# Decay levels of the third block: affine step of the forget gate inside the logarithm, row copy one place forward, signed differences

## The chip, the cores and the metric

The kernel runs on one core of a Trainium2 chip. The metric is the device time of one execution in microseconds; before the change it is 2814.32 us (median of 3 runs, 2813.81 to 2816.1).

## The reference, cut to what matters

Three model blocks run one after the other over 1024 tokens of width 1024. The change lies in the HGRN2 mixer of the third: four heads, each 128 channels by 1024 tokens.

```python
forget = lbf + (1.0 - lbf) * jax.nn.sigmoid(f_pre)
log_f = jnp.log(forget)
k = 1.0 - forget
b = jnp.cumsum(log_f, axis=2)                     # inside a chunk
diff = b[:, :, :, None, :] - b[:, :, None, :, :]
decay = jnp.exp(jnp.where(causal[:, :, None], diff, -jnp.inf))
scores = jnp.einsum('bhtd,bhsd,bhtsd->bhts', qc, kc, decay)
o = jnp.einsum('bhts,bhse->bhte', scores, vc) + jnp.einsum('bhtd,bhde->bhte', qc * jnp.exp(b), S)
S = jnp.exp(b_last) * S + jnp.einsum('bhsd,bhse->bhde', kc * jnp.exp(b_last - b), vc)
```

The decay depends on the channel, so the scores are not one plain matmul. The kernel works with chunks of 128 tokens and splits the pairs (query t, key s) by levels. At level j the tokens fall into groups of 2m, m = 2^j. A key in the first half of a group meets a query in its second half through the pivot, the last token of the first half: exp(b[t]-b[s]) = exp(b[t]-pivot) * exp(pivot-b[s]). Both exponents are at most zero.

## The kernel before, in words

The third block multiplies h3 (1024 tokens) by its weights in 16 channel tiles, called windows w = 0 to 15 here. A window is 16 steps of three matmuls (lines 369 to 371: high by high, low by high, high by low part), each 128x128 by 512. Its result is copied out of PSUM by ScalarE with Copy, Silu or Sigmoid (line 2614). Window 5 + 2h yields the sigmoid of head h, tile `p3[FT3 + h]`. ScalarE then makes the high part of the weights of window w + 2 (`high`, line 2569) and GpSimd the low part (`low`, line 2410).

From window 7 on, TensorE puts one item of the decay work after every third step, five to a window. The items are listed in `items`: for each of the four heads "diag", the levels 0 to 6, "end" and "start", 40 in all. Level 0 has m = 1 and level 6 has m = 64. I call the point of TensorE's order at which item n stands its slot. Each engine goes through the items in an order written out in the code, with semaphores between them:

- VectorE, loop of lines after `cumulate(0)`: for n = 0, 1, ... it does `difference(n)` (line 2704), `queries_decayed(n - 1)` (line 2718: query half times its exponential) and `merge(n - 3)` (lines 2728 and 2736: the scores in PSUM are copied by mask into `score`). In the turn of level 6 it also does `forget` of the next head (lines 2676 and 2681) and in the turn of "start" `cumulate` (line 2687, eight prefix sums of 128 tokens).
- ScalarE: in window w it does `exponents(n)` for five items, two ahead of TensorE's: a pass Abs (line 2576) and a pass Exp with scale -1 (line 2578) over the same tile `dec_e`. After the first of them comes the logarithm (line 2607) of the next head. `rows` (line 2591) copies the transposed keys of "end" from PSUM over the head's decay tile. Then it waits for the end of the window and does line 2614 and `high`.
- GpSimd: `low`, then `keys_decayed(n)` (line 2421: key half times its exponential).
- TensorE: `level(n)` (line 2466 for levels, 2464 for "diag", 2462 for the transposes of "end"). It waits for the keys, the queries and, since items n and n - 2 use the same PSUM pair, for `merge(n - 2)`, and after an "end" for `rows`.

`dec_e` has four buffers (`difference(n)` waits for the matmuls of item n - 4), `qe` has three.

```python
nc.scalar.activation(e, e, ACT.Abs).then_inc(abs_ok, 1)
act.wait_ge(abs_ok, upto(n, has_diff))
nc.scalar.activation(e, e, ACT.Exp, scale=-1.0).then_inc(exp_ok, 1)
```

Of the kernel before, what the change touches and what calls it, by code (L numbers as in the profile page):

```python
# [10 lines left out]
ACT = mybir.ActivationFunctionType  # L11
ALU = mybir.AluOpType
# [3 lines left out]
P = 128  # L16
S = 1024
# [61 lines left out]
def build(nc, a, out):  # L79
# [4 lines left out]
    def sem(name):  # L84
        held.append(nc.alloc_semaphore(name))
        return held[-1]
# [14 lines left out]
    with top:  # L101
# [2183 lines left out]
        def first_of_third(sp):  # L2285
            for n in range(2):
# [10 lines left out]
                    bias=(at(169, "bo2", [P, D]), a["b_out2"]),  # L2297
# [6 lines left out]
        p3 = at(16, "p3", [P, 2 * KT, S])  # L2304
# [4 lines left out]
        lbs = at(4.25, "lbs", [P, 8, 4])  # L2309
# [12 lines left out]
        kT3 = at(128, "kT3", [P, 2, S])  # L2322
# [14 lines left out]
        QT, FT3, GT = 4, 8, 12  # L2337
        N_T3, N_J3, LOOK, PER_TILE = 2 * KT, 3 * KT, 2, 5
        kinds = ["diag"] + list(range(LEVELS)) + ["end", "start"]
        items = [(h, kind) for h in range(HEADS) for kind in kinds]  # L2340
        N_ITEM3, FIRST_WINDOW = len(items), 7

        def upto(n, which):
            return sum(which(kind) for _, kind in items[:max(0, n + 1)])

        is_level = lambda kind: isinstance(kind, int)
        has_diff = lambda kind: is_level(kind) or kind == "end"
# [26 lines left out]
        def half_slot3(x, n):  # L2374
# [3 lines left out]
        p3_lbs, tile3_mm, p3_out, w3_hi, w3_lo, i_mm, i_out = (sem(x) for x in (  # L2378
            "p3_lbs", "tile3_mm", "p3_out", "w3_hi", "w3_lo", "i_mm", "i_out"))
        c3_in, win_step, lb_dve, lb_act = sem("c3_in"), sem("win_step"), sem("lb_dve"), sem("lb_act")  # L2380
        zero_ok, forget_ok, ln_ok, cum_ok = sem("zero_ok"), sem("forget_ok"), sem("ln_ok"), sem("cum_ok")
        diff_ok, abs_ok, exp_ok, qe_ok, ke_ok, lv_mm, merged, rows_ok = (sem(x) for x in (
            "diff_ok", "abs_ok", "exp_ok", "qe_ok", "ke_ok", "lv_mm", "merged", "rows_ok"))
        el_ok, o3_mm, st3_mm, st3_ok, sq3_ok, sd3_ok, on3_ok, ot3_mm, y3_ok, own3 = (sem(x) for x in (
            "el_ok", "o3_mm", "st3_mm", "st3_ok", "sq3_ok", "sd3_ok", "on3_ok", "ot3_mm", "y3_ok", "own3"))
        pool_mm, pool_ok = sem("pool_mm"), sem("pool_ok")
# [5 lines left out]
        with nc.Block() as block:  # L2392
# [47 lines left out]
            def _(pe):  # L2440
                def level(n):
                    h, kind = items[n]
                    if not has_mm(kind):
                        return
                    bank = pair[2 + n % 2]
                    if upto(n - 2, is_score):
                        pe.wait_ge(merged, upto(n - 2, is_score))
                    ends = upto(n - 2, lambda x: x == "end")
                    if ends:
                        pe.wait_ge(rows_ok, ends)  # L2450
                    if kind == "diag":
                        pe.wait_ge(forget_ok, 2 * h + 2)
                    else:
                        pe.wait_ge(ke_ok, upto(n, has_diff))
                    if is_level(kind):
                        pe.wait_ge(qe_ok, upto(n, by_q))
                    e = dec_e[:, n % N_DEC, :]
                    for c in range(TT):
                        tok = slice(c * P, (c + 1) * P)
                        o = bank[:, c // 4, c % 4 * P:(c % 4 + 1) * P]  # L2460
                        if kind == "end":
                            last = nc.tensor.transpose(o, e[:, tok], ident[:])
                        elif kind == "diag":
                            last = nc.tensor.matmul(o, kT3[:, h % 2, tok], queries(n)[:, tok], start=True, stop=True)
                        else:
                            last = nc.tensor.matmul(bank[:, 0, c * 64:(c + 1) * 64], e[:, tok],
                                                    qe[:, n % N_QE, c * 64:(c + 1) * 64], start=True, stop=True)
                    last.then_inc(lv_mm, 1)
# [24 lines left out]
                for w in range(2, N_T3):  # L2493
                    pe.wait_ge(w3_lo, w + 1)
                    pe.wait_ge(p3_out, w - 1)
                    for i in range(2 * KT):
                        tile_step(w, i)
                        n = PER_TILE * (w - FIRST_WINDOW) + i // 3
# [63 lines left out]
            def _(act):  # L2562
# [8 lines left out]
                def exponents(n):  # L2571
                    h, kind = items[n]
                    e = dec_e[:, n % N_DEC, :]
                    if has_diff(kind):
                        act.wait_ge(diff_ok, upto(n, has_diff))
                        nc.scalar.activation(e, e, ACT.Abs).then_inc(abs_ok, 1)
                        act.wait_ge(abs_ok, upto(n, has_diff))
                        nc.scalar.activation(e, e, ACT.Exp, scale=-1.0).then_inc(exp_ok, 1)
                    elif kind == "start":
                        act.wait_ge(cum_ok, h + 1)  # L2580
                        b = decay(n)
                        nc.scalar.activation(elast[:, h, :], b.rearrange("p (c s) -> p c s", s=P)[:, :, P - 1],
                                             ACT.Exp).then_inc(el_ok, 1)
                        act.wait_ge(lv_mm, upto(n - N_DEC, has_mm))
                        nc.scalar.activation(e, b, ACT.Exp).then_inc(exp_ok, 1)

                def rows(n):
                    act.wait_ge(lv_mm, upto(n, has_mm))
                    act.wait_ge(el_ok, head_of(n) + 1)
                    act.wait_ge(exp_ok, upto(n + 1, has_exp))  # L2590
                    nc.scalar.activation(decay(n), flat(pair[2 + n % 2]), ACT.Copy).then_inc(rows_ok, 1)
# [8 lines left out]
                for w in range(N_T3):  # L2600
                    h = (w - 6) // 2
                    starts = w >= 6 and w % 2 == 0 and h < HEADS
                    todo = items_in(w)
                    for i, n in enumerate(todo):
                        if starts and (h == 0 and i == 0 or h and i == 1):
                            act.wait_ge(forget_ok, 2 * h + 2)
                            nc.scalar.activation(p3[:, FT3 + h, :], p3[:, FT3 + h, :], ACT.Ln).then_inc(ln_ok, 1)
                        exponents(n)
                        if n >= 3 and items[n - 3][1] == "end":
                            rows(n - 3)  # L2610
                        if n == N_ITEM3 - 1:
                            rows(n - 1)
                    act.wait_ge(tile3_mm, w + 1)
                    nc.scalar.activation(p3[:, P3_ORDER[w], :], flat(p3_pair(w)),
                                         (ACT.Copy, ACT.Silu, ACT.Sigmoid, ACT.Silu)[P3_ORDER[w] // 4]).then_inc(p3_out, 1)
                    high(w + 2)
# [6 lines left out]
                for c in range(TT):  # L2623
# [9 lines left out]
                    if c < 4:  # L2633
                        act.wait_ge(pool_mm, c + 1)
                        nc.scalar.activation(y3T[:, c, :], flat(pair[3]), ACT.Copy,
                                             scale=col("pool_scale", c)).then_inc(pool_ok, 1)

            @block.vector
            def _(dve):
                second_out[3](dve)  # L2640
                own = Count(dve, lb_dve)
# [9 lines left out]
                own.then(nc.vector.reciprocal(lbs[:, 4, :], lbs[:, 3, :]))  # L2651
                own.then(nc.vector.tensor_tensor(lbs[:, 5, :], lbs[:, 1, :], lbs[:, 4, :], ALU.mult))
                own.then(nc.vector.tensor_scalar(lbs[:, 6, :], lbs[:, 5, :], -1.0, 1.0, ALU.mult, ALU.add))
                step = Count(dve, win_step)
                dve.wait_ge(c3_in, 48)
                for g, w in enumerate(POOL_WINDOWS):
                    x = p3[:, g, :]
                    dve.wait_ge(p3_out, g + 1)
                    step.then(nc.vector.tensor_copy(win[0][:, 16:], x))
                    m, i = 1, 0  # L2660
                    while m < w:
                        step.then(nc.vector.tensor_tensor(win[1 - i][:, 16:], win[i][:, 16:],
                                                          win[i][:, 16 - m:16 + S - m], ALU.add))
                        m, i = 2 * m, 1 - i
# [8 lines left out]
                def forget(h):  # L2673
                    f = p3[:, FT3 + h, :]
                    dve.wait_ge(p3_out, 6 + 2 * h)
                    nc.vector.tensor_scalar(f, f, lbs[:, 6, h:h + 1], lbs[:, 5, h:h + 1], ALU.mult,
                                            ALU.add).then_inc(forget_ok, 1)
                    dve.wait_ge(forget_ok, 2 * h + 1)
                    if h >= 2:
                        dve.wait_ge(lv_mm, upto((h - 1) * len(kinds) - 1, has_mm))  # L2680
                    nc.vector.tensor_scalar(kT3[:, h % 2, :], f, -1.0, 1.0, ALU.mult, ALU.add).then_inc(forget_ok, 1)

                def cumulate(h):
                    f = p3[:, FT3 + h, :]
# [9 lines left out]
                def difference(n):  # L2694
                    h, kind = items[n]
                    if not has_diff(kind):
                        return
                    m = 1 << kind if is_level(kind) else P
                    size = 2 * m if is_level(kind) else P
                    b = decay(n).rearrange("p (c s) -> p c s", s=size)  # L2700
                    e = dec_e[:, n % N_DEC, :].rearrange("p (c s) -> p c s", s=size)
                    if upto(n - N_DEC, has_mm):
                        dve.wait_ge(lv_mm, upto(n - N_DEC, has_mm))
                    nc.vector.tensor_tensor(e, b, b[:, :, m - 1:m].broadcast_to([P, S // size, size]),
                                            ALU.subtract).then_inc(diff_ok, 1)

                def queries_decayed(n):
                    h, kind = items[n]
# [34 lines left out]
                for n in range(N_ITEM3 + 3):  # L2743
# [6 lines left out]
                    h, i = (n + 3) // len(kinds), (n + 3) % len(kinds)  # L2750
# [986 lines left out]
def rows(w):  # L3737

    k, n = w.shape
    return np.ascontiguousarray(w.reshape(k // P, P, n).transpose(1, 0, 2))  # L3740
# [101 lines left out]
```

## Time and profile before

| what | value |
|---|---|
| median of 3 runs | 2814.32 us |
| profiled execution, its time | 2812.37 us |
| its span | 2810.5 us |
| TensorE busy | 2706.1 us, 96% |
| VectorE busy | 2108.7 us, 75% |
| ScalarE busy | 1035.8 us, 37% |
| GpSimd busy | 489.2 us, 17% |
| mean granted TensorE clock | 0.991 |

TensorE is busy nearly all the time over the whole span. The busy time of a matmul is modelled: matmuls overlap, so that one of 0.39 us follows the one before after 0.23 us. What is worth reading are the stretches in which TensorE is idle, and how far apart its pieces of work start. The decay items run from 1810 us to 1969 us.

### The profile page before, as it was taken

The numbers are of one execution on the slowest core, as the hardware profiler recorded it, in microseconds if no ns is written. First come the engines' busy times: TensorE is split into PE (matmuls) and PEld (weight loads), VectorE is DVE, ScalarE is ACT, GpSimd is POOL, SyncE is SP. The second block draws the span as 40 slices with busy tenths as digits, with TensorE's granted clock in tenths as the row PEclk, the third lists the DMA queues.
The fourth block names the chain that finished last, engine by engine and source line by source line (L and its number), as shares of the span: only waits on it lengthen the run. The fifth ranks groups of instructions, "written<-read, shape, count | busy, mean of one in ns | idle before, by whom it ended". The sixth has DMA issues, their size and how long they took to land. (4 is left out here: it accounts for less than half of the span.)

```text
span 2810.5 us, 33531 instructions
## 1 busy us (share of the span) xinstructions
PE 2706.1 (96%) x13192; PEld 2204.2 (78%) x13192; DVE 2108.7 (75%) x2827; ACT 1035.8 (37%) x1500; POOL 489.2 (17%) x260
## 2 busy tenths in 40 slices
PE   6999999999999999899999899999999999999998
PEld 5888888888888878488776578878878788888887
DVE  6999997864724672599977876688186988887978
ACT  5111112142414332422127641477231555545332
POOL 0000000000100011002220100345120466665000
PEclk8999999999999999999999999999999999999999
DMA  5212322233335551011110032110122222224431
GB/s 222 113 61 74 107 81 62 90 109 122 111 107 170 151 164 53 31 61 45 46 57 2 31 126 96 39 31 20 57 107 88 83 83 90 75 90 165 188 98 60
DMA packets 97567, 250.19 MB, mean 89 GB/s; under 512 B 7345, under 2 KB 34353, under 8 KB 95746
## 3 DMA queue, kind: packets, MB, share of 16 engines
q1 hardware_dynamic: 92866, 231.49, 24.2%
q10 hardware_dynamic: 4288, 15.73, 1.4%
q8 instruction: 105, 1.72, 0.3%
q0 software_dynamic: 256, 0.82, 0.1%
q14 instruction: 52, 0.43, 0.1%
HBM read 202.92 MB, written 45.09 MB: 88 GB/s over the span
## 5 line engine op out<-in xcount | busy, mean ns | idle before, releaser
L369 PE MATMUL pair<-u_hi,w_hi 128*128 128x512 f32 x768 | 302.1, 393 | 1.2 <-PEq L92 0.9
L640 DVE SCALAR_TENSOR_TENSOR conv_acc<-aT,cols,conv_acc 128x1024 f32<-128x1024 f32 x232 | 297.8, 1283 | 6.7
L370 PE MATMUL pair<-u_lo,w_hi 128*128 128x512 f32 x768 | 300.2, 391 | 0.0
L371 PE MATMUL pair<-u_hi,w_lo 128*128 128x512 f32 x768 | 300.1, 391 | 0.0
L369 PEld LDWEIGHTS pair<-u_hi,w_hi 128*128 128x128 f32 x768 | 145.1, 189 | 32.6 <-issue 2.4
L1867 DVE TENSOR_SCALAR_CACHE_REDUCE counted<-choice,top_i 128x384 uint8<-128x384 f32 (+2 forms) x192 | 169.2, 941 | 0.0
L370 PEld LDWEIGHTS pair<-u_lo,w_hi 128*128 128x128 f32 x768 | 145.1, 189 | 30.6 <-issue 0.7
L371 PEld LDWEIGHTS pair<-u_hi,w_lo 128*128 128x128 f32 x768 | 145.0, 189 | 30.6
L369 PE MATMUL pair<-h_hi,ch_hi 128*128 128x512 f32 x392 | 155.4, 396 | 2.2 <-ACT ch L1763 2.0
L370 PE MATMUL pair<-h_lo,ch_hi 128*128 128x512 f32 x392 | 153.2, 391 | 0.0
L371 PE MATMUL pair<-h_hi,ch_lo 128*128 128x512 f32 x392 | 153.1, 391 | 0.0
L1013 POOL TENSOR_TENSOR yrT<-yrT,gate_c 128x1024 f32<-128x1024 f32 x8 | 18.9, 2369 | 758.2 <-ACT yrT L906 758.2
L3033 POOL TENSOR_TENSOR op_lo<-w_sum,op_hi 128x512 fp32r<-128x512 f32 x80 | 137.0, 1713 | 34.2 <-ACT op_hi L3163 34.2
L1652 POOL TENSOR_TENSOR ch_lo<-wt,ch_hi 128x1024 fp32r<-128x1024 f32 x17 | 40.9, 2404 | 526.4 <-ACT ch_hi L1611 526.4
L453 DVE TENSOR_TENSOR w_lo<-wt,w_hi 128x1024 fp32r<-128x1024 f32 (+1 forms) x64 | 69.8, 1090 | 77.1 <-ACT w_hi L449 77.1
L3083 PE MATMUL pair<-t_hi,op_hi 128*128 128x512 f32 x320 | 124.6, 389 | 0.1
L3085 PE MATMUL pair<-t_lo,op_hi 128*128 128x512 f32 x320 | 124.5, 389 | 0.0
L3086 PE MATMUL pair<-t_hi,op_lo 128*128 128x512 f32 x320 | 124.5, 389 | 0.0
L449 ACT ACTIVATE w_hi<-wt 128x1024 fp32r<-128x1024 f32 (+1 forms) x64 | 60.8, 950 | 142.8 <-PE pair L371 135.1
L1272 DVE TENSOR_TENSOR wo_lo<-wo_raw,wo_hi 128x1024 fp32r<-128x1024 f32 x44 | 54.1, 1229 | 66.7 <-ACT wo_hi L1401 66.6
L369 PE MATMUL pair<-h_hi,p_hi 128*128 128x512 f32 x256 | 103.5, 404 | 0.0
L371 PE MATMUL pair<-h_hi,p_lo 128*128 128x512 f32 x256 | 100.2, 391 | 0.0
(497 smaller groups left out, 7041.0 us busy)
## 6 DMA issues: line engine op xcount, KB each, us to landing
wt<-in_w_ch SPq DMA_DIRECT2D x60, 512.0 KB, 3.4
wo_raw<-in_w_out SPq DMA_DIRECT2D x44, 512.0 KB, 3.6
wt<-in_w_up SPq DMA_DIRECT2D x10, 1024.0 KB, 4.9
w_raw<-in_w_up SPq DMA_DIRECT2D x10, 1024.0 KB, 4.9
g_spill<-g_stage SPq DMA_DIRECT2D x40, 256.0 KB, 2.2
ada_mod<-in_ada_mod SPq DMA_DIRECT2D x4, 2048.0 KB, 14.4
wt<-in_w_conv SPq DMA_DIRECT2D x16, 512.0 KB, 3.5
qk<-qk_st SPq DMA_DIRECT2D x8, 1024.0 KB, 6.4
```

The source lines that it names most:

```text
L369: nc.tensor.matmul(bank, w[0], x[0], start=(first and k == 0), stop=False)
L370: nc.tensor.matmul(bank, w[0], x[1], start=False, stop=False)
L371: return nc.tensor.matmul(bank, w[1], x[0], start=False, stop=(last and k == n_k - 1))
L449: nc.scalar.activation(slot_view(w_parts[0], n), slot_view(wt, n), ACT.Copy).then_inc(job_hi, 1)
L453: nc.vector.tensor_tensor(slot_view(w_parts[1], n), slot_view(wt, n), slot_view(w_parts[0], n).bitcast(F32), ALU.subtract).then_inc(job_lo, 1)
L640: nc.vector.scalar_tensor_tensor(dst, x, w, conv_acc[:], ALU.mult, ALU.add).then_inc(conv_step, 1)
L1272: nc.vector.tensor_tensor(wo_parts[1][:, n % 2, :], wo_raw[:, n % 2, :], wo_parts[0][:, n % 2, :].bitcast(F32), ALU.subtract).then_inc(wo_ ...
L1867: nc.vector.tensor_scalar(counted[:, t % 2, 0:w], scores(t), least, None, op, ALU.add, accum_out=found[:, t - 2:t - 1]).then_inc(counts_ok, 1)
L3033: nc.gpsimd.tensor_tensor(op_lo[j], operand(w, j), op_hi[j].bitcast(F32), ALU.subtract).then_inc(op_lo_ok, 1)
L3083: nc.tensor.matmul(bank, hi[:, k, :], x_hi[:, k, :], start=(j in opens and k == 0), stop=False, skip_group_check=True)
L3085: nc.tensor.matmul(bank, hi[:, k, :], x_lo[:, k, :], start=False, stop=False, skip_group_check=True)
L3086: last = nc.tensor.matmul(bank, lo[:, k, :], x_hi[:, k, :], start=False, stop=(k == 3), skip_group_check=True)
```

## The change

- `forget` no longer writes the forget gate back. It computes only the keys, k = 1 - forget, as one affine step of the sigmoid with two columns per head (a new column `lbs[:, 7]` is the negative of `lbs[:, 6]`). The affine step of the forget gate itself is the scale and bias of the logarithm's activation.
- `rows` of the item "end" stands after the exponents two items later instead of three.
- `difference` writes the two halves of a group with separate instructions: pivot minus b for the keys' half, b minus pivot for the queries' half. "end" has the first only, over whole chunks. So the Abs pass goes, and Exp is taken without a scale.

```diff
@@ TensorE, level(n)
                     if kind == "diag":
-                        pe.wait_ge(forget_ok, 2 * h + 2)
+                        pe.wait_ge(keys_ok, h + 1)
@@ ScalarE, exponents(n)
                         act.wait_ge(diff_ok, upto(n, has_diff))
-                        nc.scalar.activation(e, e, ACT.Abs).then_inc(abs_ok, 1)
-                        act.wait_ge(abs_ok, upto(n, has_diff))
-                        nc.scalar.activation(e, e, ACT.Exp, scale=-1.0).then_inc(exp_ok, 1)
+                        nc.scalar.activation(e, e, ACT.Exp).then_inc(exp_ok, 1)
@@ ScalarE, windows
                         if starts and (h == 0 and i == 0 or h and i == 1):
-                            act.wait_ge(forget_ok, 2 * h + 2)
-                            nc.scalar.activation(p3[:, FT3 + h, :], p3[:, FT3 + h, :], ACT.Ln).then_inc(ln_ok, 1)
+                            act.wait_ge(keys_ok, h + 1)
+                            nc.scalar.activation(p3[:, FT3 + h, :], p3[:, FT3 + h, :], ACT.Ln, bias=lbs[:, 5, h:h + 1],
+                                                 scale=lbs[:, 6, h:h + 1]).then_inc(ln_ok, 1)
                         exponents(n)
-                        if n >= 3 and items[n - 3][1] == "end":
-                            rows(n - 3)
+                        if n >= 2 and items[n - 2][1] == "end":
+                            rows(n - 2)
@@ VectorE
                 own.then(nc.vector.tensor_scalar(lbs[:, 6, :], lbs[:, 5, :], -1.0, 1.0, ALU.mult, ALU.add))
+                own.then(nc.vector.tensor_scalar(lbs[:, 7, :], lbs[:, 6, :], -1.0, None, ALU.mult))
@@ VectorE, forget(h)
-                    nc.vector.tensor_scalar(f, f, lbs[:, 6, h:h + 1], lbs[:, 5, h:h + 1], ALU.mult,
-                                            ALU.add).then_inc(forget_ok, 1)
-                    dve.wait_ge(forget_ok, 2 * h + 1)
                     if h >= 2:
                         dve.wait_ge(lv_mm, upto((h - 1) * len(kinds) - 1, has_mm))
-                    nc.vector.tensor_scalar(kT3[:, h % 2, :], f, -1.0, 1.0, ALU.mult, ALU.add).then_inc(forget_ok, 1)
+                    nc.vector.tensor_scalar(kT3[:, h % 2, :], f, lbs[:, 7, h:h + 1], lbs[:, 6, h:h + 1], ALU.mult,
+                                            ALU.add).then_inc(keys_ok, 1)
@@ VectorE, difference(n)
-                    nc.vector.tensor_tensor(e, b, b[:, :, m - 1:m].broadcast_to([P, S // size, size]),
-                                            ALU.subtract).then_inc(diff_ok, 1)
+                    pivot = b[:, :, m - 1:m].broadcast_to([P, S // size, m])
+                    keys = nc.vector.tensor_tensor(e[:, :, 0:m], pivot, b[:, :, 0:m], ALU.subtract)
+                    if is_level(kind):
+                        keys = nc.vector.tensor_tensor(e[:, :, m:size], b[:, :, m:size], pivot, ALU.subtract)
+                    keys.then_inc(diff_ok, 1)
```

## Rows read from the trace of the kernel before

**Rows 1.** Busy time by stretch: us, then each engine's busy time (x instructions), clock.

```profile
1860.40:1902.00 41.60, 38.20 (x232) 32.79 (x232) 35.96 (x35) 31.28 (x30) 20.43 (x11) 1.00 0.09 26
1943.60:1967.50 23.90, 23.88 (x153) 21.42 (x154) 23.59 (x18) 16.07 (x16) 13.39 (x7) 1.00 0.04 12
1967.50:2000.00 32.50, 32.50 (x149) 26.97 (x147) 0.00 (x0) 7.29 (x9) 5.77 (x5) 1.00 0.11 34
```

**Rows 2.** TensorE's waits, 1700 to 2060 us: total us, times, longest.

```profile
PE pair L2466 <- POOL dec_e L2421: 2.7, 3, 0.9
PE pair L2462 <- POOL dec_e L2421: 2.6, 3, 0.9
PE pair L2466 <- DVE score L2736: 2.4, 3, 0.8
PE pair L2464 <- issue: 2.4, 3, 0.8
...
PE pair L2466 <- DVE score L2728: 0.4, 1, 0.4
```

**Rows 3.** TensorE's items of head 1 and two of head 2, in order of time.

```profile
1868.29 1.89 PE L2466 MATMUL pair<-qe,dec_e 128*128 128x64 f32 x16
1872.84 1.89 PE L2466 MATMUL pair<-qe,dec_e 128*128 128x64 f32 x16
1876.71 1.89 PE L2466 MATMUL pair<-qe,dec_e 128*128 128x64 f32 x16
1881.54 2.00 PE L2466 MATMUL pair<-qe,dec_e 128*128 128x64 f32 x16 [0.80 <-DVE score L2736]
1886.52 1.06 PE L2462 MATMUL pair<-ident,dec_e 128*128 128x128 f32 x8 [0.86 <-POOL dec_e L2421]
1893.19 2.02 PE L2464 MATMUL pair<-p,kT 128*128 128x128 f32 x16 [0.82 <-issue]
...
1902.06 1.97 PE L2466 MATMUL pair<-qe,dec_e 128*128 128x64 f32 x16 [0.90 <-POOL dec_e L2421]
```

**Rows 4.** Instructions by line: duration in ns, minimum, median and maximum, first and last start.

```profile
L2704 DVE TENSOR_TENSOR dec_e<-p x32: 1201/1272/3393, 1805.2 to 1957.6; 128x1024 f32<-128x1024 f32 x32
L2576 ACT ACTIVATE dec_e<-dec_e x32: 1043/1057/1065, 1806.5 to 1961.0; 128x1024 f32<-128x1024 f32 x32
L2718 DVE TENSOR_TENSOR qe<-p,dec_e x28: 677/693/1772, 1810.0 to 1960.9; 128x512 f32<-128x512 f32 x28
L2578 ACT ACT_TABLE_LOAD  x12: 1283/1283/1283, 1807.6 to 1958.4; - x12
L2676 DVE TENSOR_SCALAR p<-p,lbs x4: 811/2866/2874, 1798.9 to 1916.0; 128x1024 f32<-128x1024 f32 x4
L2681 DVE TENSOR_SCALAR kT<-p x4: 694/694/694, 1799.8 to 1918.9; 128x1024 f32<-128x1024 f32 x4
L2736 DVE COPY_PREDICATED score<-masks,pair x28: 697/730/1321, 1821.3 to 1966.6; 128x512 f32<-128x512 int32 x28
L202 ACT ACTIVATE xT<-xT,msum,g x8: 1224/1228/1233, 29.4 to 58.0; 128x1024 f32<-128x1024 f32 x8
```

**Rows 5.** ScalarE in order of time, head 0.

```profile
1815.47 1.06 ACT L2578 ACTIVATE dec_e<-dec_e 128x1024 f32<-128x1024 f32 x1
...
1830.73 1.02 ACT L2614 ACTIVATE p<-pair 128x1024 f32<-128x1024 f32 x1
```

**Rows 6.** VectorE in order of time, heads 0 and 1.

```profile
1840.63 4.76 DVE L2687 TENSOR_TENSOR_SCAN p<-ones_col,p 128x128 f32<-128x128 f32 x8
...
1862.92 1.31 DVE L2736 COPY_PREDICATED score<-masks,pair 128x512 f32<-128x512 int32 x1
...
1872.16 1.77 DVE L2718 TENSOR_TENSOR qe<-p,dec_e 128x512 f32<-128x512 f32 x1
```

**Rows 7.** GpSimd in order of time, heads 0 and 1.

```profile
1832.78 2.42 POOL L2410 TENSOR_TENSOR p_lo<-wt,p_hi 128x1024 fp32r<-128x1024 f32 x1 [0.98 <-ACT p_hi L2569]
...
1871.08 2.30 POOL L2421 TENSOR_TENSOR dec_e<-kT,dec_e 128x512 f32<-128x512 f32 x1 [1.13 <-ACT dec_e L2578]
```

More of the change, by code:

```diff
@@ L2380, in build @@
         c3_in, win_step, lb_dve, lb_act = sem("c3_in"), sem("win_step"), sem("lb_dve"), sem("lb_act")
-        zero_ok, forget_ok, ln_ok, cum_ok = sem("zero_ok"), sem("forget_ok"), sem("ln_ok"), sem("cum_ok")
-        diff_ok, abs_ok, exp_ok, qe_ok, ke_ok, lv_mm, merged, rows_ok = (sem(x) for x in (
-            "diff_ok", "abs_ok", "exp_ok", "qe_ok", "ke_ok", "lv_mm", "merged", "rows_ok"))
+        zero_ok, keys_ok, ln_ok, cum_ok = sem("zero_ok"), sem("keys_ok"), sem("ln_ok"), sem("cum_ok")
+        diff_ok, exp_ok, qe_ok, ke_ok, lv_mm, merged, rows_ok = (sem(x) for x in (
+            "diff_ok", "exp_ok", "qe_ok", "ke_ok", "lv_mm", "merged", "rows_ok"))
         el_ok, o3_mm, st3_mm, st3_ok, sq3_ok, sd3_ok, on3_ok, ot3_mm, y3_ok, own3 = (sem(x) for x in (
```

## The prediction

> **What bounds the kernel now.** First the page: TensorE is busy 96% of the span, so only what shortens TensorE's idle time or its work can move the end. Then the stretches [rows 1]. In one head's period of decay items (1860.4 to 1902.0 us) TensorE is busy 38.20 of 41.60 us. Before and after the items it is not idle at all: 32.50 of 32.50 us right behind them. The clock is 1.00 in these stretches, so no clock is to be won. In the same period VectorE is busy 35.96 us, ScalarE 31.28 and GpSimd 20.43. The waits [rows 2] put a bound on the whole change: TensorE waits 2.7 + 2.6 + 2.4 + 2.4 + 0.4 = 10.5 us in 13 places, and nowhere else among the decay items.
>
> The true price of a wait is read from the distances of the slots [rows 3]. An undisturbed item follows the one before after 3.87 us (1872.84 to 1876.71), and after 4.55 us where a window ends between them (1868.29 to 1872.84). Level 6 stands 4.83 us behind level 5: 0.96 late. "end" stands 4.98 us behind level 6: 1.11 late. "diag" stands 6.67 us behind "end", where 9 + 9 + 3 matmuls of 0.23 us (4.8) and the item's own 1.06 make 5.8: 0.85 late, and I give the item itself another 0.1 (2.02 us where 1.9 is normal). Level 1 costs 0.9 of wait and by the same refill 1.05. Together 4.05 us per head, so an undisturbed period is 37.5 us instead of 41.6. Three periods lie between level 1 of head 0 and of head 3: 12.2 us. Level 1 of head 0 has 0.4 of wait, 0.55 with refill. The last head from its level 1 on has no wait (23.88 of 23.90 busy). The most that can be had is 12.75 us.
>
> **The change part by part.** The times below are those of head 0, whose events recur 41.6 us later in head 1.
>
> *Abs pass.* It is 32 x 1.057 = 33.8 us of ScalarE [rows 4], an engine with 10 us to spare per head; as a sum it is worth nothing. Where it counts is the latency of the first items of a head. After the copy of a window and `high` comes Abs, then a table load (1.28 us), then Exp of level 1, starting at 1815.47 [rows 5]. VectorE and GpSimd both wait for it, and VectorE isn't idle again for 30 us. Without Abs the load directly follows `high` and Exp starts at 1814.41 and ends at 1815.47: 1.06 us earlier for everything behind. Table loads stay 12, as Exp still follows Copy or Ln.
>
> *Halved differences.* 28 of the 32 become two instructions of 512 elements. The trace has no such write. The nearest row is the query product, 512 elements with every second one read, 0.69 us, against 1.20 for a whole difference [rows 4]. Back to back each overlaps the next by about 0.08, so two cost 1.22 to 1.36, that is 0.05 to 0.15 more per level, and 7 x 0.1 = 0.7 us per head. The far end is `merge`: at the levels with m = 1 and 2 it takes 1.31 us for the same 512 elements, otherwise 0.70 [rows 4, 6]. If the strided write did that, levels 0 and 1 would cost 1.2 us more each, 2.4 us per head. I take the 0.1, since merge differs in more than its write (mask, PSUM). Below nothing: the halves cannot be faster than the whole, as the element count is the same.
> On this the Trainium skill, "SBUF — State Buffer", the box on SBUF cachelines, says that lines are 16 bytes and that fp32 may be strided by up to four elements without loss. By it halves with m = 1 and 2 are free of a penalty, and so should merge's writes be, at 1.31 us. By the rule the sum stays 12; with merge's price 1 to 3 us of it would go.
>
> *Two instructions, two chances to be cut off.* VectorE and GpSimd hold each other up here: a key product takes 2.30 us at 1871.08 and the query product that starts at 1872.16 takes 1.77 instead of 0.69 [rows 4, 6, 7]; the first waited for the difference, the second for the product. A halved difference lets a waiting key product in between its halves, which delays its Exp by one product (1.15 us), but the query product behind is then no longer held up. So it moves the wait, it does not add one.
> The same page of the Trainium skill ("Who interferes with whom") has it that whoever starts first holds the shared pair for its whole instruction, and that two-input instructions of VectorE take part. That speaks against the change, as it adds instructions on that pair; it is the first rival below.
>
> *Forget.* Line 2676 goes: 0.81 us alone, 2.87 beside GpSimd's `low` [rows 4]. What remains (line 2681) gets the columns as operands as 2676 had, so it costs 0.81 instead of 0.69, and it inherits the place behind `low` and its 2.87. So the gain is 0.69 us per head on VectorE, in the turn right before level 6. The extra small instruction at the start (`lbs` 7) runs on four columns once, while VectorE waits for windows: nothing; without that cover, under 0.2 us. Both ends for the keys: -0.69 and -0.6 us.
>
> *Ln with bias and scale.* An activation with both from columns takes 1.23 us (line 202) where a plain one takes 1.06 [rows 4]: +0.17 us per head on ScalarE, between Exp of level 6 and Exp of "end", where the removed Abs of "end" leaves 1.06. At worst it is 0.17 of 12.
>
> *Row copy.* It now waits right behind the Exp of "start" for the transposes of "end". Behind it on ScalarE stands Exp of the next head's level 0, whose difference comes 2 us later anyway. "diag" on TensorE waited for this copy ("issue" in [rows 2], 0.85 each); the copy stood behind level 0's Abs and Exp. That wait goes whole.
>
> **The walk through one head**, from Exp(1) ready at 1815.47, with these prices and one engine of the two held off as above. TensorE's undisturbed slots: level 1 at 1818.2, 2 at 1822.1, 3 at 1825.9, 4 at 1830.5, 5 at 1834.4, 6 at 1838.2, "end" 1842.1, "diag" of head 1 at 1848.0, level 1 of head 1 at 1855.7.
> VectorE: queries 1 and merge of "diag" to 1817.4 (TensorE needs it at 1818.2), difference 3 with a key product between its halves to 1819.8, queries 2 and merge 0 to 1821.5, difference 4 to 1823.3, queries 3 and merge 1 to 1825.0, difference 5 to 1826.8, queries 4 and merge 2 to 1828.0, difference 6 to 1830.2, queries 5 and merge 3 to 1831.4.
> ScalarE has Exp(5) done at 1827.9, then waits for the window (1828.3), copies it to 1830.2 (at 1830.73 to 1831.75 now, [rows 5]), `high` to 1831.2, Exp(6) to 1833.4.
> GpSimd does `low` from 1831.2 to 1833.6 (2.42, [rows 7]). The keys of head 1 wait for it: 1834.1. Key product 6 to 1835.3, difference of "end" to 1836.4, queries 6 and merge 4 to 1837.5. Level 6 can start at 1838.2: no wait. Merge 5 to 1838.1.
> ScalarE: Ln to 1836.0, load, Exp("end") to 1838.4 (1842.15 now). The key product of "end", 2.4 us like `low`, comes to 1841 with a scan in front: "end" at 1842.1, no wait. Prefix sums 4.76 us as now [rows 6]: 1842.9. Rows at 1843.2 to 1844.2, "diag" at 1848.0: no wait. "start" queries, merge 6, difference 0 to 1845.9; difference 1 to 1847.2; Exp(0) 1847.0; copy, `high`, load, Exp(1) of head 1 at 1852.6, three microseconds ahead of level 1's slot, as it was in head 0 (2.7).
> So every wait goes, with 0.2 to 1 us in hand at levels 1 and 6. The tightest is level 6, 0.7 us. I leave 0.75 us in all for places where it doesn't quite do: 12.0 us. The own time of the profiled execution, 2812.37 us, becomes 2800.4; the median shown is 1.95 us above it, so 2814.3 - 12.0 = 2802.3.
>
> **The rivals.**
> (A) The pair shared by VectorE and GpSimd becomes the bound. Per head, alone: differences 7 x 1.22 + 1.15, queries 7 x 0.61 + 1.15, keys 0.8, prefix sums 3.1, merges 6.5: 25.5 us of VectorE, of it 19 on the pair; GpSimd 7 x 1.15 + 2.4 + 2 x 2.4 = 15.2. That is 34.2 us of a 37.5 us period, 91%. For: little is left, and with merge's price on levels 0 and 1 it is 36.6. Against: the walk. Then a half to three quarters of the waits stay: 3 to 8 us gained, 2809 by the middle. 22%.
> (B) The engine gains are spent before TensorE sees them: POOL's latency decides at level 1 and "end". Against: ScalarE's Exp comes 1 and 4 us earlier. Gain under 3 us, or given back behind the items: 2813. 6%.
> (C) Slower: a halved difference costs as much as a whole one at every level (an instruction's price not falling with its size). Then VectorE has 7 x 1.15 = 8 us more per head on 35.96 busy of 41.6, less 0.7: 43.3, so the period grows by 1.7, in three heads 5 us: 2820. It decides from 0.95 us per half on, where the 0.69 of the query product speaks against it. 3%.
> (D) The change doesn't do what it says, for instance Exp needing more table loads: 2 or more further loads per head of 1.28 would bring ScalarE, 31.3 - 8.5 us busy, nowhere near the bound. In (B).
>
> **How the numbers follow.** Forecast 69%, its own range 2800.5 to 2805. (A) 22%, (B) 6%, (C) 3%. The range goes up to 2809 to hold most of (A), and down to 2800 (nothing beyond 12.75, and about 1.5 us for the runs). What a measurement can tell from no change is 0.2%, 5.6 us: a gain above it is the forecast, 69%, and three quarters of (A): 86%. Within it: the rest of (A), (B) and a part of (C), 11%. Slower 3%.
>
> **What would show it.** TensorE's waits on lines 2462, 2464 and 2466: under 1.5 us in all. Level 1 of head 0 to that of head 3: 112 to 113 us where it was 124.8 (three periods). No Abs; 60 differences, of 0.65 to 0.7 us alone; Ln near 1.2 us. The keys' step takes up to 2.9 us, 0.8 in head 0. Wrong: halves at levels 0 and 1 above 1.2 us, VectorE over 36 of its new period and TensorE still waiting at level 6 (then A), or a "diag" still late (then the rows' step).

## The result: 0.5% faster, more than forecast

| | before | changed |
|---|---|---|
| median of 4 runs | 2814.4 us (2813.81 to 2816.1) | 2798.69 us (2798.33 to 2800.32) |
| profiled execution | 2812.37 us | 2799.01 us |
| its span | 2810.5 us | 2796.6 us |
| TensorE busy | 2706.1 us | 2701.4 us |
| VectorE busy | 2108.7 us | 2102.8 us |
| ScalarE busy | 1035.8 us | 1003.9 us |

The ratio is 0.9947, 95% interval 0.9932 to 0.9962. The gain is 15.7 us by the medians, 13.9 us by the spans. The forecast was 12.0 us and 2802.3, range 2800.0 to 2809.0: the direction came out and so did the mechanism in the main; the time lies 1.3 us below the range, for reasons given behind the experiments.

The stretches of two heads, columns as in [rows 1]:

```profile
1855.30:1892.60 37.30, 37.30 (x233) 33.15 (x233) 34.73 (x41) 23.32 (x22) 19.41 (x10) 1.00 0.10 29
1892.60:1929.90 37.30, 37.30 (x234) 33.14 (x233) 34.72 (x41) 23.33 (x22) 18.50 (x11) 1.00 0.09 29
```

A head now takes 37.3 us instead of 41.6, and TensorE is busy in all of it, where it had 38.20 of 41.60 [rows 1]. ScalarE went from 31.3 to 23.3 us per head. VectorE went only from 36.0 to 34.7, so its share rose from 86% to 93%. TensorE's waits of the changed kernel from 1700 to 2060 us answer [rows 2]: no line of the decay items (2462, 2464, 2466) is left. The waits that are listed stand behind the items and are in the kernel before too, where they come 14 us later, so that part of them falls outside the window of [rows 2].

```profile
PE pair L2524 <- DVE y3T L2768: 3.1, 2, 2.7
PE pair L2543 <- DVE state L2778: 1.7, 2, 0.8
PE pair L369 <- PEq L2392: 1.1, 1, 1.1
```

TensorE's items of head 1 in order of time, which answer [rows 3]:

```profile
1863.08 1.89 PE L2466 MATMUL pair<-qe,dec_e 128*128 128x64 f32 x16
1867.63 1.89 PE L2466 MATMUL pair<-qe,dec_e 128*128 128x64 f32 x16
1871.50 1.89 PE L2466 MATMUL pair<-qe,dec_e 128*128 128x64 f32 x16
1875.37 1.89 PE L2466 MATMUL pair<-qe,dec_e 128*128 128x64 f32 x16
1879.23 1.03 PE L2462 MATMUL pair<-ident,dec_e 128*128 128x128 f32 x8
1884.91 1.95 PE L2464 MATMUL pair<-p,kT 128*128 128x128 f32 x16
```

Level 6 follows level 5 after 3.87 us (4.83 before), "end" after 3.86 (4.98), "diag" after 5.68 (6.67). No item stands late. The distance from the start of the first "diag" to the start of the last "end" is the measure used from here on; I call it the stretch. "Late" means: by these distances, against the changed kernel. The stretch was 1967.58 - 1810.48 = 157.1 us and is 1953.78 - 1810.37 = 143.4 us: 13.7 us, which is the 13.9 us of the spans to within 0.2.

The changed instructions by line answer [rows 4] (ns: minimum, median, maximum):

```profile
L2703 DVE TENSOR_TENSOR dec_e<-p x32: 665/983/3393, 1804.9 to 1943.2; 128x512 f32<-128x512 f32 x28, 128x1024 f32<-128x1024 f32 x4
L2705 DVE TENSOR_TENSOR dec_e<-p x28: 674/682/1781, 1805.5 to 1940.3; 128x512 f32<-128x512 f32 x28
L2576 ACT ACTIVATE dec_e<-dec_e x32: 1040/1060/1066, 1806.2 to 1946.5; 128x1024 f32<-128x1024 f32 x32
L2576 ACT ACT_TABLE_LOAD  x12: 1283/1283/1283, 1802.2 to 1943.0; - x12
L2678 DVE TENSOR_SCALAR kT<-p,lbs x4: 787/813/2756, 1798.8 to 1905.5; 128x1024 f32<-128x1024 f32 x4
```

A half takes 0.67 to 0.69 us when nothing holds it up, the keys' step 0.79 to 0.81, and the table loads are still 12. VectorE at the levels 0 (two halves) and 1 (two halves) of head 1:

```profile
1843.35 0.68 DVE L2703 TENSOR_TENSOR dec_e<-p 128x512 f32<-128x512 f32 x1
1843.94 0.69 DVE L2705 TENSOR_TENSOR dec_e<-p 128x512 f32<-128x512 f32 x1
1844.55 0.69 DVE L2703 TENSOR_TENSOR dec_e<-p 128x512 f32<-128x512 f32 x1
1845.15 0.69 DVE L2705 TENSOR_TENSOR dec_e<-p 128x512 f32<-128x512 f32 x1
```

With m = 1 and m = 2 a half costs no more than at the other levels. The Trainium skill, "SBUF — State Buffer", the box on SBUF cachelines, says that fp32 can be strided by up to four elements for free; for these differences (0.68 to 0.69 us) the trace agrees. Merge's 1.31 us at the same two levels (1.30 in the changed kernel too) has another cause, which no run here separates.

The margin in front of the items is not the same in each head. The key product of level 1 is over 3.05, 1.88, 1.20 and 0.75 us ahead of its item in heads 0 to 3. No wait came of it in four heads; whether the margin would settle or run out in a fifth is not shown.

### The profile page after: what moved, and what is told of

Read it like the earlier page. It is cut to its first block and busy times, and to the rows that moved or that the text cites. A ratio compares the mean times of both kernels' runs of the same rounds, so it can differ in the third digit from the quotient of the medians.

```text
span 2796.6 us, 33524 instructions
## 1 busy us (share of the span) xinstructions
PE 2701.4 (97%) x13192; PEld 2204.8 (79%) x13192; DVE 2102.8 (75%) x2852; ACT 1003.9 (36%) x1468; POOL 485.8 (17%) x260
```

## The experiments

Two theories stood against each other. Theory 1: all waits hang on one chain, the latency of Exp on ScalarE, so the Abs pass gives nearly everything. Theory 2: each edit takes away a wait of its own. All edits were built singly and left out singly, eight kernels with the two ends. All stretches are from one profiled execution each; those of the two ends were profiled again further down. The single edits "rows" and "forget" move the median by 0.08%, and the intervals of their ratios reach 1.0001: by the times alone they can't be told from no change, and only the stretch tells them.

| edits in the kernel | stretch, us | against before | median, us | before, same chip |
|---|---|---|---|---|
| none | 157.1 | 0 | 2814.4 | |
| rows | 154.4 | -2.7 | 2811.54 | 2813.99 |
| forget | 154.8 | -2.3 | 2811.8 | 2813.99 |
| Abs with halves | 147.4 | -9.7 | 2804.07 | 2813.99 |
| rows, forget | 152.1 | -5.0 | 2808.3 | 2813.54 |
| forget, Abs with halves | 145.6 | -11.5 | 2802.25 | 2813.54 |
| rows, Abs with halves | 144.7 | -12.4 | 2801.23 | 2813.54 |
| all three | 143.4 | -13.7 | 2799.3 | 2813.99 |
| all three, Abs pass kept | 155.7 | -1.4 | 2811.9 | 2813.54 |

**Signed halves without Abs, alone.** Forget and rows stay as before.

```diff
-nc.scalar.activation(e, e, ACT.Abs).then_inc(abs_ok, 1)
-act.wait_ge(abs_ok, upto(n, has_diff))
-nc.scalar.activation(e, e, ACT.Exp, scale=-1.0).then_inc(exp_ok, 1)
+nc.scalar.activation(e, e, ACT.Exp).then_inc(exp_ok, 1)
...
-nc.vector.tensor_tensor(e, b, b[:, :, m - 1:m].broadcast_to([P, S // size, size]), ALU.subtract)
+keys = nc.vector.tensor_tensor(e[:, :, 0:m], pivot, b[:, :, 0:m], ALU.subtract)
+if is_level(kind):
+    keys = nc.vector.tensor_tensor(e[:, :, m:size], b[:, :, m:size], pivot, ALU.subtract)
```

> Only the signed differences in halves and the removal of Abs; forget in two steps and the row copy three items later stay. Theory 1 (the latency of Exp on ScalarE is what every wait hangs on): nearly all of the 13.7 us between the items' ends goes, period 37.3 to 38 us, gain 11 to 14 us; at most level 6 keeps a wait, since VectorE's second affine step stays. Theory 2 (each edit removes its own wait: rows that of diag, forget that of level 6, Abs those of level 1 and end): gain about 3 x 2.2 + 0.6 = 7 us, waits on lines 2464 and at level 6 stay.

Ratio 0.9963 (0.995 to 0.9977). The stretch lost 9.7 us, between the two theories. TensorE's waits among the items:

```profile
PE pair L2464 <- issue: 1.7, 2, 0.8
PE pair L2466 <- DVE score L2737: 0.7, 2, 0.4
```

Up to level 5 of head 1 nothing waits; in heads 1 and 2 level 6 waits 0.4 us (VectorE) and the "diag" behind it 0.8 (the row copy), 0.5 and 1.0 late by the distances. What is left belongs to the other two edits, and the waits on key products (5.3 us in [rows 2]) are gone. But in head 0 this edit alone also took away the waits of level 6 and of "diag", and half of that of level 6 later on, which theory 2 gave to the other two.

**Forget alone.**

```diff
-nc.vector.tensor_scalar(f, f, lbs[:, 6, h:h + 1], lbs[:, 5, h:h + 1], ALU.mult, ALU.add)
-dve.wait_ge(forget_ok, 2 * h + 1)
-nc.vector.tensor_scalar(kT3[:, h % 2, :], f, -1.0, 1.0, ALU.mult, ALU.add)
+nc.vector.tensor_scalar(kT3[:, h % 2, :], f, lbs[:, 7, h:h + 1], lbs[:, 6, h:h + 1], ALU.mult, ALU.add)
```

> Only the affine step inside the logarithm. VectorE has 0.69 us less per head in front of level 6. Theory 1: the waits of diag and level 1 stay at 0.85 to 1.05 each, level 6 and end lose 0.7 each: gain 2 to 4 us. Theory 2: level 6 loses its wait, nothing else: 2 us.

Ratio 0.9992 (0.9982 to 1.0001): 2.3 us in the stretch. TensorE's waits:

```profile
PE pair L2462 <- POOL dec_e L2421: 3.5, 3, 1.2
PE pair L2466 <- POOL dec_e L2421: 2.7, 3, 0.9
PE pair L2464 <- issue: 1.5, 3, 0.5
PE pair L2466 <- DVE score L2736: 0.2, 1, 0.2
PE pair L2466 <- DVE score L2728: 0.2, 1, 0.2
```

Level 6 is late by 0.3 us instead of 0.96, "diag" lost a third, but "end" waits longer (3.5 for 2.6): counted from level 5, TensorE arrives there 0.7 us sooner, the key product only 0.4. Theory 1 had "end" lose 0.7 per head, and theory 2 had level 6 lose its wait and nothing else change; neither came out.

**Rows alone.**

```diff
-if n >= 3 and items[n - 3][1] == "end":
-    rows(n - 3)
+if n >= 2 and items[n - 2][1] == "end":
+    rows(n - 2)
```

> Only the row copy one place forward. ScalarE sits idle 5 us there now, so the copy leaves the chain copy of window, high, Abs, Exp(1) by 1.0 us. Theory 1 and 2 both: the wait of diag goes, 2.6 us. Theory 1 adds that level 1, whose Exp comes 1.0 us earlier, loses its wait as well: 5 to 6 us, with the waits of level 6 and end unchanged or smaller.

Ratio 0.9992 (0.9983 to 1.0001): 2.7 us. "diag" stands 5.7 us behind "end" and waits no more, but level 1 now waits 1.05 each time instead of 0.90. Counted from "end", Exp of level 1 does come 0.9 us sooner, but TensorE, no longer held up at "diag", comes 1.1 sooner. Both theories had the first part; the second part of theory 1 failed.

**Two of three.** The three kernels with one edit put back.

> The changed kernel with the row copy back at three items later. Alone the three edits shortened the stretch from the first diag to the last end by 9.7 (Abs and signed halves), 2.3 (forget) and 2.7 us (rows), 14.6 together against 13.7 for all. If each edit takes away its own wait, diag is late again by 0.9 us in two or three heads: the stretch is 145.2 to 146.1 us instead of 143.4. If the Abs pass alone freed the chain (theory 1), the copy ends at 1846.8 in head 0, in front of the slot of diag at 1847.6, and nothing is lost: 143.4.

Ratio 0.9959 (0.9945 to 0.9974): stretch 145.6, 2.2 us lost. "diag" waits in heads 1 to 2 and 2 to 3 (0.33 and 0.81), not from head 0 to 1. The lateness there is 0.5 and 1.0 us. Of the two things expected, the first (145.2 to 146.1): each its own wait, though from head 0 to 1 nothing is lost.

> The changed kernel with forget in two affine steps and the plain logarithm. Own wait (theory 2): level 6 is late by 0.4 to 0.5 us in heads 1 and 2, as in abs_only: 144.3 us. Theory 1: VectorE sits idle 1.4 + 1.2 us in front of level 6's merge in head 0 of the changed kernel, so 0.7 us more there costs nothing: 143.4 to 143.6.

Ratio 0.9955 (0.994 to 0.997): stretch 144.7, 1.3 us lost, half of it at level 6 of head 2 (0.5 late), the rest at level 1 of heads 2 and 3 (0.2 and 0.3) and the items behind. Level 6 of head 1, which I had in the sum, was in time. The loss is 0.4 us more than the first theory's 144.3 and sits in part elsewhere; the second (nothing lost) is out for head 2, and holds for head 1.

> Only forget and rows: the kernel before with these two, whole differences and the Abs pass. Alone they gave 2.3 and 2.7 us. Theory 2: 5 us, stretch 152.1 us. Theory 1: with both out of the way Abs costs less than the 9.7 us it gave alone, so more than 5 us: 148 to 151 us. Waits of level 1 and end, both on the key product behind Exp, remain in either.

Ratio 0.9981 (0.9972 to 0.9991): stretch 152.1, to the tenth what theory 2 had worked out from the single edits (157.1 - 2.3 - 2.7). TensorE's waits on key products (end 3.5, level 1 2.3 us) remain. So theory 1, by which Abs gives nearly everything, is out. The single gains sum to 14.6 us against 13.7 together, and what an edit is worth depends little on the others: rows 2.2 to 2.7, forget 1.3 to 2.3, Abs with halves 8.7 to 9.7. That the waits are separate, as theory 2 had it, holds only roughly: its 7 us for the Abs edit were 9.7, and each of the edits also moved a wait that was not its own.

**The Abs pass kept.** This splits the third edit: signed halves stay, and Abs is put in front of Exp again.

> The changed kernel with an Abs pass in front of each Exp, as before: signed halves, forget and rows stay. Against no_abs_edit this isolates the halves, against the changed kernel the pass. If the pass is what held TensorE up, the stretch is as in no_abs_edit plus up to 1 us per head for the halves' 0.1 to 0.15 us each (rival A: halves cost on the pair shared with GpSimd). If halves help, because a waiting key product gets in between them, it is shorter than no_abs_edit.

Ratio 0.9994 (0.9984 to 1.0003): stretch 155.7 us. Against rows and forget with whole differences (152.1) it is 3.6 us longer, against the changed kernel 12.3 us. TensorE's waits:

```profile
PE pair L2462 <- POOL dec_e L2421: 6.5, 3, 2.4
PE pair L2466 <- POOL dec_e L2421: 0.3, 1, 0.3
PE pair L2466 <- DVE score L2731: 0.2, 1, 0.2
```

These are 7.0 us, where the kernel with whole differences has 6.0. The longer waits sit at "end", and they start earlier. VectorE's difference of level 5 in head 0, with halves and Abs:

```profile
1824.70 1.38 DVE L2705 TENSOR_TENSOR dec_e<-p 128x512 f32<-128x512 f32 x1
1826.01 0.68 DVE L2707 TENSOR_TENSOR dec_e<-p 128x512 f32<-128x512 f32 x1
```

and with whole differences and Abs:

```profile
1828.38 1.26 DVE L2704 TENSOR_TENSOR dec_e<-p 128x1024 f32<-128x1024 f32 x1
```

The first half was held up by a key product (1.38 for 0.68 us). Counted from each kernel's first "diag" (1808.80 and 1813.10), the difference is over at 17.9 us with halves and at 16.5 whole, 1.35 later. ScalarE passes that on through its copy of the window, `high`, the logarithm and four table loads, without a pause: Exp("end") is over at 32.55 against 31.2, again 1.35, and TensorE's "end" starts at 35.1 against 33.85. The last passes with halves:

```profile
1837.94 1.04 ACT L2576 ACTIVATE dec_e<-dec_e 128x1024 f32<-128x1024 f32 x1
1839.00 1.28 ACT L2578 ACT_TABLE_LOAD   x1
1840.29 1.06 ACT L2578 ACTIVATE dec_e<-dec_e 128x1024 f32<-128x1024 f32 x1
```

So "end" waits 2.4 us in head 0. What costs more is what follows it: TensorE's granted clock falls to 0.50, that is from 2.4 to 1.2 GHz, behind the waits at "end" in heads 0 and 2 (2.37 and 2.19 us), and not behind that in head 1 (1.98 us). Two stretches of the kernel with the pass, then its "end" of head 0, then the same item with whole differences:

```profile
1843.60:1847.00 3.40, 3.08 (x12) 2.82 (x13) 3.40 (x5) 1.10 (x2) 0.17 (x1) 0.50 0.03 7
1925.50:1928.90 3.40, 3.29 (x12) 3.03 (x13) 3.40 (x6) 1.31 (x2) 0.00 (x0) 0.50 0.02 5
```

```profile
1843.92 1.94 PE L2462 MATMUL pair<-ident,dec_e 128*128 128x128 f32 x8 [2.37 <-POOL dec_e L2421]
```

```profile
1846.95 1.06 PE L2462 MATMUL pair<-ident,dec_e 128*128 128x128 f32 x8 [1.16 <-POOL dec_e L2421]
```

The next "diag" stands 7.16 and 7.28 us behind these two "end" items, where 5.68 is undisturbed: 1.48 and 1.60 us more, and no wait is recorded in them, only slower matmuls. The kernel with whole differences has no such fall among its items. So about 3.0 of the 3.6 us are the clock's, which fell only behind the longest waits, and 0.6 the longer waits themselves. The 12.3 us that the pass costs contain the same 3.1.

**More pieces.** How much does the changed kernel have in hand on VectorE? Each half is issued as four, then eight instructions over the same elements.

```diff
+parts = 4 if is_level(kind) else 1        # 8 in the second kernel
+step = S // size // parts
+for j in range(parts):
+    g = slice(j * step, (j + 1) * step)
+    keys = nc.vector.tensor_tensor(e[:, g, 0:m], pivot[:, g, :], b[:, g, 0:m], ALU.subtract)
...
```

> The changed kernel with every half difference issued as four instructions of 128 elements: the same elements, 84 + 84 more instructions that share the pair with GpSimd. At about 0.2 us from one to the next this adds some 2.5 us of VectorE per head and three more gaps per half for a waiting key product. If the pair is as near to its bound as rival A counted (91 to 92% of a 37.3 us period), waits come back: stretch 145 to 151 us. If the changed kernel has the 3 us in hand in front of level 6 that its trace shows, 143.4 to 145.

Ratio 0.9978 (0.9969 to 0.9988) to before's 2812.3 on the same chip: median 2806.55, stretch 150.35, 6.9 us lost to 168 more instructions.

> The same with eight instructions of 64 elements per half. At about 0.13 us each that is 6 us more of VectorE per head, above the slack of any engine count: waits in every head under either theory, stretch 150 to 165 us. The pair of runs gives the price per added instruction and the point from which halving would have lost.

Ratio 1.0027 (1.0016 to 1.0038): median 2819.82, stretch 165.0 (1810.50 to 1975.47), 21.6 us lost to 392 more. Slower than before the change. VectorE's pieces in the two kernels (ns):

```profile
L2711 DVE TENSOR_TENSOR dec_e<-p x112: 275/279/300, 1807.6 to 1951.0; 128x128 f32<-128x128 f32 x112
```

```profile
L2711 DVE TENSOR_TENSOR dec_e<-p x224: 205/212/220, 1806.1 to 1963.9; 128x64 f32<-128x64 f32 x112
```

and four pieces of one half in a row, in the first of the two kernels:

```profile
1819.69 0.88 DVE L2711 TENSOR_TENSOR dec_e<-p 128x128 f32<-128x128 f32 x4
```

Alone, 512 elements take 0.68, 128 take 0.28, 64 take 0.21 us: 0.14 us per instruction and 1.05 ns per element. In a row they overlap, so four pieces take 0.88 us where the half takes 0.68: 0.07 us of VectorE for each added instruction. TensorE loses 0.041 us for each with four pieces and 0.055 with eight. The difference is the clock again: with eight pieces the granted clock stands at 0.5 three times among the items (from 1842.9, 1887.3 and 1945.3 us), with four never. The items there are late by about 6.3 us in which nobody waits (my estimate, from the same items of the heads without a fall). Without them it is 15.3 us, 0.039 for each.

Head 0 stays free of waits with four pieces; from "diag" of head 1 on the periods are 39.5 and 39.9 us instead of 37.3. The margin of 3 us in head 0 is not there in heads 1 and 2, where the changed kernel has 1.88 and 1.20. The waits are on key products and on merges. The first is level 0 of head 1, whose key product took 4.05 us, against 1.26 alone:

```profile
1849.59 4.05 POOL L2421 TENSOR_TENSOR dec_e<-kT,dec_e 128x512 f32<-128x512 f32 x1 [6.84 <-ACT dec_e L2576]
```

VectorE ran eight pieces and a query product in a row until 1852.25 meanwhile, and the gaps between them did not let it in. So what rival A described is near: a few instructions more on the engines that hold each other up, and waits come back. That the pair is the bound then is not shown, as VectorE is busy 36.9 of 39.9 us in such a period and itself waits for ScalarE.

**The kernel before again, twice,** with a profile, and the changed kernel once more.

> The changed kernel once more, for the size of its gain against the kernel before on the same chip. From the items' ends in the two traces (1967.58 and 1953.78 us) 13.8 us; the medians differ by 15.7 us. If the 2 us between are only how the runs scatter, the gain here is 13 to 15 us; if something outside the items is faster too, it is 15 to 17 us and the traces show where.

2799.3 us (2798.42 to 2799.72, 5 runs) against 2813.99 (21 runs): ratio 0.9944 (0.9932 to 0.9957), 14.7 us; stretch 1810.59 to 1954.00, again 143.4.

> The kernel before, one more execution with a profile. Its profiled execution (2812.37 us) lay below the median of its runs by 1.6 to 2 us. If the waits among the decay items differ from one execution to the next, the stretch from the first diag to the last end is other than 157.1 us, by as much as the time differs from 2812.4. If the scatter comes from elsewhere, the stretch is 157.1 again.

> As before_b, a third profiled execution of the kernel before: stretch and time move together if the waits are what scatters, and the changed kernel, which has no wait there, scatters less (2798.4 to 2800.3 us in nine runs against 2811.0 to 2817.7).

| execution of before | time | first diag | last end | stretch |
|---|---|---|---|---|
| first | 2812.37 | 1810.48 | 1967.58 | 157.10 |
| second | 2817.74 | 1814.36 | 1971.47 | 157.11 |
| third | 2812.56 | 1810.61 | 1967.73 | 157.12 |

The stretch repeats to 0.02 us while the time moves by 5.4 us, 3.9 of it ahead of the first item. So of the two possibilities it is the second: the scatter lies outside the changed stage. Much of it goes with TensorE's granted clock. Ahead of the first item the second execution has 51.2 us at 0.5, the other two 44.4 us each; at half speed the 6.8 us more cost 3.4 of the 3.9 (an estimate). The runs agree: of the 21 of before on one chip the nine with a mean clock of 0.991 took 2812.8 us on average, the ten with 0.990 took 2815.1. All but one of the changed kernel's nine runs were at 0.991. Why, and whether that is chance, stays open; the four runs of the Abs edit alone spread over 5.7 us.

## Why the prediction came out as it did

**What bounds it, and that waits are the whole prize:** right. Stretch and span shortened by nearly the same, 13.7 and 13.9 us, and nothing was given back behind the items.

**"The most that can be had is 12.75 us":** the step that failed, a term of the sum that was mis-sized. The waits gave 13.7. The period without waits was put at "37.5 us instead of 41.6", 4.05 per head; measured 37.27 against 41.57, 4.30. Term by term: "diag" was 0.99 late, where I wrote 0.85, because the 5.8 us that I summed for the way to it are 5.68; the items right behind a wait also start 0.07 to 0.1 late, which I counted only once. That is 0.25 per head; between head 0 and head 1 the distance holds 0.2 more, mostly because the levels 2 and 3 of head 0 start 0.1 late too. I had both numbers in the rows and rounded each against the change.

**The 0.75 us held back** "for places where it doesn't quite do": there was none. Together 1.7 of the 1.9 us by which the 12.0 fall short of the spans' 13.9.

**From the profiled execution to the median:** the second term that failed, and the larger one. "The median shown is 1.95 us above it" was carried over as a constant; in the changed kernel the median lies 0.3 us below the profiled execution. That is 2.3 of the 3.6 us between 2802.3 and 2798.69; the sum of the waits, 12.0 for 13.4 by the times of the two profiled executions, is the other 1.4. As far as the runs tell this is scatter and no step of the mechanism: before's profiled execution lay below its four runs and the changed kernel's among its own. The repeat with 21 and 5 runs has 14.7 us where the first medians had 15.7. The lower end of the range, 12.75 us and 1.5 for the runs, was built on the first error; with 13.7 it would have been 2799.1, still 0.4 us above the result. So the mechanism was right in the main, its size too small by 1 us, and the rest of the distance to the range luck with the runs.

**Abs pass.** "1.06 us earlier for everything behind" was too small. Level 0's Exp now goes ahead of the window's copy by more than its Abs, because its table load runs during the wait for the difference. ScalarE in head 0 of the kernel before:

```profile
1806.50 1.06 ACT L2576 ACTIVATE dec_e<-dec_e 128x1024 f32<-128x1024 f32 x1 [4.40 <-DVE dec_e L2704]
1807.58 1.28 ACT L2578 ACT_TABLE_LOAD   x1
```

and of the changed kernel:

```profile
1802.19 1.28 ACT L2576 ACT_TABLE_LOAD   x1
1806.21 1.07 ACT L2576 ACTIVATE dec_e<-dec_e 128x1024 f32<-128x1024 f32 x1 [2.73 <-DVE dec_e L2705]
1807.29 1.28 ACT L2613 ACT_TABLE_LOAD   x1
1808.58 1.03 ACT L2613 ACTIVATE p<-pair 128x1024 f32<-128x1024 f32 x1
1809.51 1.05 ACT L2569 ACTIVATE p_hi<-p_raw 128x1024 fp32r<-128x1024 f32 x1
1810.58 1.28 ACT L2576 ACT_TABLE_LOAD   x1
1811.87 2.01 ACT L2576 ACTIVATE dec_e<-dec_e 128x1024 f32<-128x1024 f32 x2
```

Exp(1) starts at 1811.87, where it was 1815.47 [rows 5]: 3.6 us, of which two Abs passes are 2.1, the load that no longer stands between Abs and Exp 1.3 and a difference ready sooner 0.3. The walk had 1814.41. This is head 0; counted from "diag", Exp of level 1 comes 3.5, 2.8, 2.1 and 1.6 us sooner in heads 0 to 3. The walk looked at one head and had the next one start with the same margin, "three microseconds ahead of level 1's slot, as it was in head 0"; measured the margin shrinks from head to head. This made the walk's margins too small (queries 6 and merge 4 were over at 1834.9, not 1837.5) but not the time, since TensorE was at its undisturbed pace in both.

**Halved differences.** The price of a pair, 1.22 us alone, was right, and merge's 1.31 rightly set aside. "So it moves the wait, it does not add one" does not hold in general: with Abs kept the halves made the waits longer by 1.0 us and the stretch by 3.6, 3.0 of it through the granted clock, a cost that the prediction had nowhere. In the changed kernel no wait came of them. What whole signed differences without Abs would give was not built.

**Forget** (0.69 us per head; level 6 came 0.67 sooner with this edit alone) and **Ln** (1.24 to 1.25 us for 1.06; forecast 1.23): right. In head 0 the keys' step came before `low` and took 0.81; the walk had them the other way round. **Row copy:** "That wait goes whole", right, and the rows' experiment shows it alone.

**Rivals.** A did not decide here. Its count, 91% of a period on the pair, was not measured: VectorE's 93% is another figure, all its instructions and the time in which GpSimd holds it up. But the margin was small, as the pieces show. C did not come (a half costs 0.69), nor B (nothing given back) or D (12 loads). Level 1 of head 0 to that of head 3 took 111.8 us, under the 112 to 113 named as the sign.

## What to carry over

Where TensorE is otherwise full, measure the distance from item to item against an undisturbed one: idle time alone gave 10.5 us here, the distances, read without rounding, 13.7. Here, where the waits had different releasers, the edits added up nearly plainly (14.6 us singly, 13.7 together), and those too small for the runs (2.3 and 2.7 us) could be told by a stretch of the trace that repeats to 0.02 us. An instruction split in two is paid from slack: no wait came of it next to a ScalarE pass removed, and 3.6 us without that. Look at the granted clock before a loss is put down to waits: 3.0 of these 3.6 us, and about 6 of the 21.6 with eight pieces, are slow matmuls behind a longer wait, and a margin that shrinks from head to head shows in no list of waits.

## What was not expected of the hardware

- ScalarE's table load is issued ahead of the wait of the activation that needs it: 1802.19 for an Exp at 1806.21. A pass that needs no table of its own, put between, kept that load from being hidden.
- Over three executions of one kernel the decay items took 157.10, 157.11 and 157.12 us while the whole moved by 5.4 us.
- Masked copies of 512 elements take 1.30 us at m = 1 and 2 and 0.70 from m = 4 on, while the differences with the same strides do not slow down.
- Behind a wait of 2.37 and one of 2.19 us TensorE's granted clock fell to 0.50 and the item and those after it took 3.1 us more in the two places; behind one of 1.98 us in the same kernel it did not.
